# Sixteen of the 22 feed-forward activation tiles split into high and low parts while the input products still run

## The reference

```python
def conv_ffn(x, w_in, conv_w, conv_b, w_out):
    h = x @ w_in
    ...
    h = lax.conv_general_dilated(h, conv_w[:, None, :].astype(h.dtype), window_strides=(1,),
                                 padding=[(CONV_W - 1, 0)],
                                 dimension_numbers=('NWC', 'WIO', 'NWC'),
                                 feature_group_count=c) + conv_b
    u, g = jnp.split(h, 2, axis=-1)
    return (jax.nn.silu(g) * u) @ w_out

    x = x + conv_ffn(rms_norm(x, ffn_norm[l]), w_ffn_in[l], ffn_conv_w[l], ffn_conv_b[l],
                     w_ffn_out[l])
```

## Time and profile before

| | us |
|---|---|
| median of 3 runs | 2270.09 |
| lowest and highest run | 2260.78, 2275.44 |
| profiled execution | 2257.7 |
| its span, first to last instruction | 2256.0 |
| PE busy in the span | 2062.7 |
| DVE, ACT, POOL busy | 1179.8, 693.6, 728.8 |

### The profile page before, as it was taken

The page is one execution under the profiler, slowest core; times in us unless marked ns, Lnnn a source line. Parts: engine busy times, 40 slices in busy tenths (PEclk is TensorE's granted clock), DMA queues, the critical chain, the costliest instruction groups (busy, mean ns, idle before and its releaser), DMA issues.

```text
span 2256.0 us, 25177 instructions
## 1 busy us (share of the span) xinstructions
PE 2062.7 (91%) x8468; PEld 1327.4 (59%) x8469; DVE 1179.8 (52%) x1968; ACT 693.6 (31%) x1230; POOL 728.8 (32%) x1218
## 2 busy tenths in 40 slices
PE   7999889999798999889999899999998898888795
PEld 5864468888586875367888686455333445323232
DVE  7647766666746346667666844326881624111113
ACT  4328633333413317733333422120000501101010
POOL 0316866656101006776666200003660000111110
PEclk9999999999999999999999899999998998899898
DMA  4210123332223210122233123113231143799984
GB/s 170 84 41 1 41 91 106 113 117 91 74 92 120 94 50 1 38 85 94 103 112 115 61 90 107 56 58 124 89 135 42 61 182 149 296 422 424 422 328 158
DMA packets 44257, 284.17 MB, mean 126 GB/s; under 512 B 8394, under 2 KB 8650, under 8 KB 21632
## 3 DMA queue, kind: packets, MB, share of 16 engines
q1 hardware_dynamic: 34272, 254.35, 30.1%
q0 software_dynamic: 9024, 19.08, 2.2%
q10 hardware_dynamic: 864, 9.44, 1.0%
HBM read 272.68 MB, written 23.60 MB: 131 GB/s over the span
## 4 chain that ended last, share of the span: by engine, by line
PE 74%; DVE 11%; DMA 8%; ACT 3%; POOL 2%; issue 2%; SPq 0%; DVEq 0%; POOLq 0%; ACTq 0%
PE bank L798 10%; PE bank L799 10%; PE bank L800 10%; DMA experts<-in_experts 6%; PE bank L1048 4%; PE bank L1222 4%; PE bank L982 3%; PE bank L984 3%; PE bank L983 3%; PE bank L1018 2%; PE bank L1153 2%; PE bank L918 2%; PE bank L889 2%; PE bank L905 1%; DVE act_low L2093 1%
## 5 line engine op out<-in xcount | busy, mean ns | idle before, releaser
L798 PE MATMUL bank<-h_high,w_high 128*128 128x512 f32 x1056 | 418.3, 396 | 39.2 <-ACT h_high L1587 13.5
L799 PE MATMUL bank<-h_low,w_high 128*128 128x512 f32 x1056 | 415.1, 393 | 0.0
L800 PE MATMUL bank<-h_high,w_low 128*128 128x512 f32 x1056 | 414.7, 393 | 0.0
L1455 ACT ACTIVATE w_high<-extra 128x2048 fp32r<-128x2048 f32 (+1 forms) x104 | 180.5, 1736 | 355.2 <-DVE w_low L1854 355.1
L1851 DVE TENSOR_SCALAR extra<-ring 128x2048 int32<-128x2048 int32 (+1 forms) x104 | 117.9, 1133 | 287.8 <-PE bank L800 166.8
L798 PEld LDWEIGHTS bank<-h_high,w_high 128*128 128x128 f32 x1056 | 201.0, 190 | 92.3 <-issue 27.3
L800 PEld LDWEIGHTS bank<-h_high,w_low 128*128 128x128 f32 x1056 | 200.8, 190 | 42.7
L799 PEld LDWEIGHTS bank<-h_low,w_high 128*128 128x128 f32 x1056 | 201.1, 190 | 41.1
L1854 DVE TENSOR_TENSOR w_low<-ring,extra 128x2048 fp32r<-128x2048 f32 (+1 forms) x104 | 217.7, 2094 | 3.6
L1222 PE MATMUL bank<-experts,rstd 128*64 128x512 f32 x512 | 128.5, 659 | 29.0 <-DMA experts<-in_experts 28.3
L983 PE MATMUL bank<-act_low,w_high 128*128 128x512 f32 x352 | 140.7, 400 | 0.0
(11 more groups left out here) (413 smaller groups left out, 3681.8 us busy)
## 6 DMA issues: line engine op xcount, KB each, us to landing
experts<-in_experts SPq DMA_DIRECT2D x34, 2048.0 KB, 23.9
ring<-in_w_ffn_in SPq DMA_DIRECT2D x44, 1024.0 KB, 4.8
experts<-in_experts SPq DMA_DIRECT2D x34, 1024.0 KB, 21.8
ring<-in_w_ffn_out SPq DMA_DIRECT2D x32, 704.0 KB, 4.0
ring<-in_w_feature SPq DMA_DIRECT2D x14, 1024.0 KB, 4.8
ring<-in_w_rest SPq DMA_DIRECT2D x9, 1024.0 KB, 4.9
ring<-in_w_out SPq DMA_DIRECT2D x8, 1024.0 KB, 5.0
powers_d<-work POOLq DMA_DIRECT2D x16, 512.0 KB, 3.0
```

The costliest lines, as they stand in the source:

```text
L798: pe.matmul(dst, high[:, at], h_high[:, k, :], start=k == 0, stop=False)
L799: pe.matmul(dst, high[:, at], h_low[:, k, :], start=False, stop=False)
L800: return pe.matmul(dst, low[:, at], h_high[:, k, :], start=False, stop=k == KD - 1)
L1455: act.activation(w_high[par_][:, 0:words], w_part[par_][:, 0:words], ACT.Copy).then_inc(w_split, 1)
```

## The change

Sixteen tiles (`EARLY` = 5 + 11) are split while the input products still run: two in each of the turns 12 to 19, after that turn's convolution (tiles 0 and 1 in turn 12, tiles 14 and 15 in turn 19). For this the loops on DVE and ACT end after turn 11 (`LOOPED` = 12), and turns 12 to 19 are written out. Tiles 16 to 20 are split after the PE's turn 21, tile 21 after its convolution. The high parts of tiles 5 to 15 go to eleven borrowed places that hold nothing needed at that time: four of `rel` (the attention's relative bias), two of `tmp`, two of `cmix`, two in `rt`, and one of `rstd`; tiles 16 to 21 go to `h_high`, and `h` is no longer used for this. As `rel` is now read until the last output product, SP waits for that product before it loads the next layer's `rel`. The arithmetic is the same.

```diff
 SPLITS = SPLIT_OUT + BLOCKS_FFN_OUT
 H_HIGH_AT = 33
 
-EARLY = H_HIGH_AT - JF - 6
-assert EARLY + 2 * KD + 1 == JF
+IN_WORK = H_HIGH_AT - JF - 6
+EARLY = IN_WORK + 11
+LOOPED = 2 * BODY
+assert EARLY == 2 * (JF - 2 - LOOPED) and EARLY + KD >= JF
...
+
+        act_high = [act_high_first[:, n, :] for n in range(IN_WORK)] + [rel_high[:, n, :] for n in range(CH_H)]
+        act_high += [tmp_high[:, n, :] for n in range(2)] + [v[:] for v in cmix_high] + [rt_high[:, n, :] for n in range(2)]
+        act_high += [rstd_high[:]] + [h_high[:, n, :] for n in range(JF - EARLY)]
+        act_part = [work[:, (JF + 6 + n) * T:(JF + 7 + n) * T] for n in range(IN_WORK)] + [rel[:, n, :] for n in range(CH_H)]
+        act_part += tmp[2:4] + [v[:] for v in cmix] + [rt[:, 4 * n:4 * n + 4].rearrange("p a c e -> p (a c e)") for n in range(2)]
+        act_part += [rstd[:, 1, :]] + [h_part[:, n, :] for n in range(JF - EARLY)]
...
                     sp.dma_start(con2[:], a["con2"]).then_inc(con2_in, 16)
+                if l:
+                    sp.wait_ge(pe_done, done(l - 1, "ffn_out", KD - 1))
                 sp.dma_start(rel[:], a["rel"][l]).then_inc(rel_in, 16)
...
                     silu(j, l * (2 * JF) + 2 * (j + 1))
-                with act.Fori(1, JF // 2 - 1) as r:
+                with act.Fori(1, LOOPED // 2) as r:
                     for s in range(2):
                         j = r * 2 + s
                         conv_tap(j, s, r * 4 + (done(l, "ffn_in", s, 0)), r * 2 + (l * JF + (s - 1)))
@@ -1602,15 +1612,19 @@
                         act.wait_ge(act_lowered, l * JF + (n + 1))
                         act.activation(act_high[n], act_part[n], ACT.Copy).then_inc(act_split, 1)
 
+                for j in range(LOOPED, JF - 2):
+                    conv_tap(j, j % 2, done(l, "ffn_in", j, 0), l * JF + (j - 1))
+                    split_high(SPLIT_FFN + j + 2, j % 2)
+                    silu(j % 2, l * (2 * JF) + 2 * (j + 1))
+                    act_high_parts(2 * (j - LOOPED), 2 * (j - LOOPED) + 2)
                 conv_tap(JF - 2, 0, done(l, "ffn_in", JF - 2, 0), l * JF + (JF - 3))
                 split_high(SPLIT_OUT, 0, words)
                 silu(0, l * (2 * JF) + 2 * (JF - 1))
-                act_high_parts(0, EARLY)
                 conv_tap(JF - 1, 1, done(l, "ffn_in", JF - 1, 0), l * JF + (JF - 2))
                 split_high(SPLIT_OUT + 1, 1, words)
-                act_high_parts(EARLY, EARLY + KD)
+                act_high_parts(EARLY, JF - 1)
                 silu(1, l * (2 * JF) + 2 * JF)
-                act_high_parts(EARLY + KD, JF)
+                act_high_parts(JF - 1, JF)
...
 
-                with dve.Fori(0, JF // BODY) as r:
+                with dve.Fori(0, LOOPED // BODY) as r:
                     for s in range(BODY):
...
 
-                for j in range(JF // BODY * BODY, JF - 2):
+                for j in range(LOOPED, JF - 2):
                     dve.wait_ge(pe_done, done(l, "ffn_in", j, 1))
                     split(j + 2, j + 2)
                     conv_rest(j, j)
+                    split_act(2 * (j - LOOPED), 2 * (j - LOOPED) + 2)
                 dve.wait_ge(pe_done, done(l, "ffn_in", JF - 2, 1))
                 split_out(0)
                 conv_rest(JF - 2, JF - 2)
-                split_act(0, EARLY)
 
                 dve.wait_ge(pe_done, done(l, "ffn_in", JF - 1, 1))
                 split_out(1)
-                split_act(EARLY, EARLY + KD)
+                split_act(EARLY, JF - 1)
                 conv_rest(JF - 1, JF - 1)
-                split_act(EARLY + KD, JF)
+                split_act(JF - 1, JF)
```

More of the change, by code:

```diff
@@ L366, in build @@
         gdiff = sb("gdiff", [P, 3])
+        rstd_high = second_names(("before_rstd_high", [P, T], F32), ("rstd_high", [P, T], F32R))[1]
         rstd = sb("rstd", [P, 2, T])
@@ L372, in build @@
         w_high = second_names(("before_w_high", [P, 6 * T], F32), *[(f"w_high{n}", [P, SLOT], F32R) for n in range(2)])[1:]
+        rel_high, _, tmp_high = second_names(("rel_high", [P, CH_H, T], F32R), ("between_highs", [P, 10 * T], F32),
+                                             ("tmp_high", [P, 2, T], F32R))
         extra = sb("extra", [P, (4 + 1 + 1 + EXTRA_PROBS) * T + P * NQ * (NQ + 1) // 2])
@@ L381, in build @@
         h_high = second_names(("before_h_high", [P, H_HIGH_AT * T], F32), ("h_high", [P, KD, T], F32R))[1]
-        act_low, act_high_last, _, act_high_first = second_names(
-            ("act_low", [P, JF, T], F32R), ("act_high_last", [P, T], F32R), ("between", [P, 5 * T], F32),
-            ("act_high_first", [P, EARLY, T], F32R))
+        act_low, _, act_high_first = second_names(
+            ("act_low", [P, JF, T], F32R), ("between", [P, 6 * T], F32), ("act_high_first", [P, IN_WORK, T], F32R))
         work = sb("work", [P, 22 * 1024])
@@ L420, in build @@
         vpow = sb("vpow", [P, 9, 2, ST])
+        cmix_high = second_names(*[(f"cmix_high{n}", [P, T], F32R) for n in range(2)])
         cmix = [sb(f"cmix{n}", [P, ST * SPC]) for n in range(2)]
[L424 to L427, removed]
+        (rt_high,) = second_names(("rt_high", [P, 2, T], F32R))
+        rt = sb("rt", [P, 9, NQ, NE])
+        act_high = [act_high_first[:, n, :] for n in range(IN_WORK)] + [rel_high[:, n, :] for n in range(CH_H)]
[4 more added lines that the diff above has]
+        act_part += [rstd[:, 1, :]] + [h_part[:, n, :] for n in range(JF - EARLY)]
         sum_tiles = [work[:, (JF + 1 + n) * T:(JF + 2 + n) * T] for n in range(5)]
@@ L464, in build @@
         chosen = work[:, 44 * T - 2 * NQ * (P + LISTS):]
-        rt = sb("rt", [P, 9, NQ, NE])
         bmat = extra[:, 16 * T:18 * T].rearrange("p (a c n) -> p a c n", a=YT, c=2)
```

## The result

| | before | with the change |
|---|---|---|
| median, lowest to highest, us | 2266.68, 2260.78 to 2275.44 (4 runs) | 2236.8, 2235.7 to 2247.55 (4 runs) |
| ratio to before, 95% interval | | 0.9879, 0.9851 to 0.9906 |
| the same kernel, run again later | 2268.51 (17 runs) | 2246.55 (6 runs), ratio 0.9916, 0.9896 to 0.9936 |
| profiled execution, us | 2257.7 | 2237.7 |

What follows compares the result with a forecast made beforehand. DVE, still splitting tiles when the PE wants them, was taken to set the pace at the first output products. Gain 31.6 us less 3.4 for POOL gives 28.2; 2270.1 - 28.2 = 2242 us, range 2226 to 2260.

Steps and rivals of the forecast that it cites:

- The bound and the chain behind the switch: After the PE's turn 21, DVE sets the start of m = 1; its chain becomes 17.4 us with the change.
- What was late next: Ahead of m = 1, the PE still waits 2.4 us for DVE, against 2.2 us before.
- The turns: In turns 12 to 19, two added tiles make DVE's turn 10.0 us, covered by the PE's 10.88 us.
- The sign on record for the first rival: DVE's mask rows in turns 13 to 20 starting without idle time ahead would show DVE as the pace.
- the first rival: In turns 12 to 19, tiles at 1.90 us make DVE the pace; time 2251 us, chance 0.17.
- the cover: In the turns, DVE may lag 5.2 us before the PE stops, as weights for turn 21 are ready early.
- The written-out turns and the wait of SP at nothing: Writing out loop turns on DVE and ACT, and SP's wait ahead of loading `rel`, were put at no cost.
- The uncertain term, POOL: In DVE's tail, POOL's overlap may cost up to 3.4 us a layer; the middle, one layer's worth, was taken.
- The 31.6 us: Gain from m = 1 starting earlier, 16.5 us in the first layer and 15.1 in the second; the upper bound.
- the lower bound: Gain of 24.8 us if POOL's overlap costs DVE's tail 3.4 us in each of the two layers.
- Everything behind m = 1 keeps its length: Stages after the first output product of m = 1 were to shift earlier with the PE, their lengths unchanged.
- The rival that time comes back later: A later stage that doesn't shift, such as the experts' loads, returns the gain; time 2270 us, chance 0.08.

Runs made afterwards that it cites:

- both: Changed kernel with tiles 16 and 17 split in turn 20 and POOL's last table of each layer behind output tile m = 0; ratio 0.9816.
- later table: POOL's last table of each layer put behind output tile m = 0; ratio 0.9951 on the kernel before, 0.9862 on the changed kernel.
- five early: Kernel before with its first five tiles split in turns 18 and 19 instead of behind turn 20; ratio 0.9951.
- four tiles a turn: Changed kernel with the 16 tiles split four a turn in turns 16 to 19 instead of two a turn in turns 12 to 19; ratio 0.9906.
- two more tiles: Changed kernel with tiles 16 and 17 also split early, in turn 20 behind its convolution, in two more free places; ratio 0.9856.

## Why the prediction was right

**The bound and the chain behind the switch: shown.** DVE sets the start of m = 1, and the pieces of its chain outside the tiles kept their length within 0.1 us: 0.20, 2.56, 4.46 and 4.01 us, for 0.20, 2.46, 4.35 and 4.01. The same sum, made for other edits ahead of their runs, gave 15.3 us (both), 17.4 (later table) and 29.1 to 31 (five early); 15.4, 17.5 and 29.6 to 30.2 were measured. What was late next was named rightly, the weights of m = 1, with 2.25 us for the expected 2.4. But tile 21, which the prediction had ready in time, was a second wait, 2.7 and 2.85 us, as POOL delayed it (with the later table that wait is gone); it lies inside the same chain and adds nothing to it, and its price came behind it, in the clock.

**The turns: shown.** No wait of the PE in turns 12 to 20, DVE late by at most 1.3 us and back within two turns. The sign on record for the first rival, DVE as the pace, did show, DVE's mask rows without idle time ahead, in turns 14, 15, 18 and 19 of both layers; but only the tiles of turns 13 and 17 met POOL's long operations (1.91 us each in turn 13), not those of all eight turns as in the rival, and the cover took it. With four tiles a turn the rival appeared, at the price that the cover of 5.2 us gives. (In the rival's sum, 11.7 - 10.88 is 0.8 and not 0.9, so DVE would be 6.6 us late and not 7.2, and the time 2250 and not 2251.)

**The written-out turns and the wait of SP at nothing: shown** for the turns (0.9995). The wait of SP was not tried alone, but the traces show no time lost by it: from the last output product of the first layer to the first of the second it is 552.6 us in the change and 554.0 before.

**The uncertain term, POOL: right in its size, wrong in what it was taken from.** The overlap costs 2.9 and 3.1 us in the tail of the change, near the bound of 3.4 in both layers, not half of it. The 31.6 us it was taken from set a stretch with POOL's overlap against a tail without it, which the later table in both kernels showed: 16.5 and 15.1 us had been read as what the change removes, but 3.5 and 2.2 us of them were POOL's overlap before. It was out of reach, as the last table was stored 5.8 us behind the PE's switch in the first layer already before the change put it back. The sum is 12.8 us a layer without POOL, 25.6, and with an overlap of like size on both sides about the same. The step gave 28.2, the stretches 25.3.

**What the prediction did not have: the clock behind the waits, and a slower rate.** Over the whole of the output products (first to last high product) the trace has 138.04 + 138.30 = 276.3 us before and 127.91 + 127.42 = 255.3 in the change: 21.0 us less, not 25.3, and less than the 24.8 that was the lower bound. "Everything behind m = 1 keeps its length" did not hold for these tiles. The change's two waits close together cost 2.8 and 2.2 us in m = 1, where before the second layer alone paid 1.6; that gives back 3.3. And each output tile from m = 2 on takes 15.05 us in place of 14.96, another 1.1 us. The view of line 992 gives the time of its matmuls by place (min/median/max in ns, then first and last start):

```profile
L992 PE MATMUL bank<-act_high_first,w_high x80: 389/389/796, 569.0 to 1365.2; 128*128 128x512 f32 x80
L992 PE MATMUL bank<-rel_high,w_high x64: 389/389/395, 572.4 to 1368.0; 128*128 128x512 f32 x64
L992 PE MATMUL bank<-rt_high,w_high x32: 392/392/393, 577.8 to 1372.1; 128*128 128x512 f32 x32
L992 PE MATMUL bank<-rstd_high,w_high x16: 397/397/397, 579.2 to 1372.8; 128*128 128x512 f32 x16
L992 PE MATMUL bank<-h_high,w_high x96: 389/393/504, 579.9 to 1376.9; 128*128 128x512 f32 x96
```

Those that read `rt_high` last 392 ns and those of `rstd_high` 397, against 389 of tiles 0 to 4 (`act_high_first`). It is not the borrowed place as such. The borrowed `rel_high` is at 389, and `h_high`, no borrowed place, is slower in half of its tiles. By tile, the three matmuls of tiles 11 to 18 take 681 to 700 ns from start to start, those of tiles 0 to 10 and 19 to 21 take 680, and before all 22 take 680. With two more tiles 16 and 17 lie elsewhere and take the same 694 and 695 ns as in `h_high`. So in these tiles it goes by the position in the order and not by the place. It begins at tile 11, the first of the second weight block and the first in `cmix_high`; the cause was not found.

**The time: near by luck in part.** 28.2 us were forecast. The output products gave 21.0, and the profiled executions differ by 20.0: the change's output products began 2.5 us later (568.97 against 566.43), 1.4 us came back between the layers, and from the last output product on both take the same, 859.2 before and 859.1. The medians differ by 29.9 and in the repetition by 22.0. The forecast added the 12.4 us by which the profiled execution before lay under its median; the change's profiled execution lies 0.9 us over its own. So 8 us too much gain and 13 us too much distance to the median made an error of 5 us. The rival that time comes back later had a chance of 0.08 and named the experts' loads; some of the time did come back, but from the clock, right behind the stretch, and none from the experts.

## What to carry over

When work that was beside another engine is moved, take that engine's price off both sides: a tail measured beside POOL is not what is removed if the new tail falls beside POOL too. When an engine has several places with slack, count its lag against the buffers behind it, and not against its own cycle: here 5 us of lag were free. And after a stall is shortened, look at how the remaining waits stand to each other; here two short ones close together cost half the clock for 4 to 5 us behind them, and 20 matmuls that nobody reads prevented it.

## What the runs showed that was not expected

The scatter between runs of one kernel goes with the granted clock. In 42 runs of the kernel before, the time falls by 13 us for each 0.01 of mean granted clock (correlation -0.96), from 2277.8 us at 0.948 to 2253.2 at 0.967. Where it falls can be seen in the profiled run of before with the later table, here beside the same window of the kernel before, whose matmuls are the same up to there:

```profile
200.00:250.00 50.00, 49.15 (x189) 25.16 (x186) 31.81 (x131) 31.98 (x105) 24.76 (x25) 0.60 0.00 0
```

```profile
200.00:250.00 50.00, 46.85 (x256) 23.81 (x252) 37.72 (x155) 40.64 (x133) 35.37 (x38) 1.00 0.02 5
```

The PE's busy time is nearly the same, 49.15 and 46.85 us, but in 189 matmuls at 0.60 in the one and in 256 at 1.00 in the other. It is in the attention, which none of the edits touches. The output products of that run start 12.3 us later (578.70 against 566.43); a matmul at 202 us starts 1.1 us later than before, and one at 276 us already the whole 12.3. Why the clock falls there in one run and not in the other was not found. This is why the stretches were compared and not the spans.
